# Latent attention scores in three f16 products, and the product with V one head later, in a hybrid attention encoder

## The reference

```python
def mixer_layer(x, c, ...):
    mod = silu(c) @ w_ada + b_ada                     # shift, scale, gate
    h = rms_norm(x, g_norm) * (1 + scale) + shift
    q_lat, kv_lat, k_rope, z_a, q_b, k_b, v_b, z_b = split(h @ w_in)
    # group A: 8 latent heads, 64 + 32 (rotary, shared key) deep, V of 64
    qa = rotate_last_32(rms_norm(q_lat, g_qa) @ w_uq)
    k_nope, va = split(rms_norm(kv_lat, g_kva) @ w_ukv)
    ka = concat(k_nope, rotate(k_rope))
    oa = softmax(qa @ ka.T * MLA_SCALE) @ va
    # group B: 8 query heads on 2 key heads of 64, q and k normalised, 2-D rotary
    ob = softmax(qb @ kb.T * GQA_SCALE) @ vb
    out = concat(oa * silu(z_a), ob * silu(z_b)) @ w_out
    return x + gate * out
```

## Time and profile before

| | |
|---|---|
| median of 3 runs | 2541.19 us (2537.12 to 2541.44) |
| the profiled execution's own time | 2537.28 us |
| its span, first to last instruction | 2535.5 us |
| mean granted TensorE clock | 0.977 of full |
| PE, DVE, ACT, POOL busy | 92%, 54%, 38%, 31% |
| key stages of q = 1 and q = 3, about | 125 and 140 us |
| tile stages of q = 1 and q = 3, 8 tiles each, about | 736 and 752 us |
| tile stages of q = 0 and q = 2, 4 tiles each, about | 304 and 238 us |

### The profile page before, as it was taken

The page is one execution under the profiler, slowest core; times in us unless marked ns, Lnnn a source line. Parts: engine busy times, 40 slices in busy tenths (PEclk is TensorE's granted clock), DMA queues, the critical chain, the costliest instruction groups (busy, mean ns, idle before and its releaser), DMA issues.

```text
span 2535.5 us, 44397 instructions
## 1 busy us (share of the span) xinstructions
PE 2341.6 (92%) x16106; PEld 1392.5 (55%) x16106; DVE 1371.3 (54%) x2444; ACT 974.1 (38%) x2202; POOL 790.5 (31%) x1325
## 2 busy tenths in 40 slices
PE   3888998899999999999989899889999999999997
PEld 1445544456556656656545455445556666665654
DVE  3645454566555555556535444446566555555563
ACT  0233333225444444444422333422354444444442
POOL 0553221664222122123036432146533113212210
PEclk7999999999999999999999999999999999999999
DMA  8712112120000000000412000132000000000001
GB/s 285 253 42 67 50 67 86 50 100 10 18 17 8 25 17 18 16 17 17 165 59 92 18 26 8 42 110 108 9 11 25 17 33 25 8 33 25 0 26 42
DMA packets 63236, 129.43 MB, mean 51 GB/s; under 512 B 6690, under 2 KB 31368, under 8 KB 63132
## 3 DMA queue, kind: packets, MB, share of 16 engines
q1 hardware_dynamic: 63136, 128.09, 14.5%
HBM read 115.44 MB, written 12.63 MB: 51 GB/s over the span
## 4 chain that ended last, share of the span: by engine, by line
PE 72%; DVE 16%; issue 5%; ACT 2%; POOL 2%; DMA 2%; SPq 1%; DVEq 0%; POOLq 0%; ACTq 0%
PE psum L600 55%; PE psum L590 10%; PE psum L808 6%; DVE region L1071 3%; DVE nmax L1054 3%; DVE hT L910 3%; ACT region L1225 1%; POOL region L1279 1%; DVE region L1029 1%; DVE KTa L872 1%; DMA Wout<-in_w_ada 1%; DVE region L1080 1%; PE psum L610 1%; PE psum L594 0%; DVE region L1031 0%
## 5 line engine op out<-in xcount | busy, mean ns | idle before, releaser
L1225 ACT ACTIVATE region<-psum 128x512 f16<-128x512 f32 x640 | 353.5, 594 | 758.5 <-PE psum L590 758.3
L600 PE MATMUL psum<-Wq,hT 128*128 128x512 f32 (+1 forms) x1536 | 611.1, 544 | 6.6 <-DVE KTa L872 5.0
L1071 DVE TENSOR_TENSOR region<-psum,region 128x512 f16<-128x512 f32 x640 | 415.7, 683 | 293.4 <-ACT region L1225 292.7
L590 PE MATMUL psum<-ident,region 128*128 128x128 f32 (+1 forms) x3208 | 436.9, 277 | 25.6 <-DVE Va L966 10.5
L600 PEld LDWEIGHTS psum<-Wq,hT 128*128 128x128 f32 x1536 | 285.0, 191 | 251.2 <-issue 224.9
L1054 DVE TENSOR_REDUCE nmax<-psum 128x1 f32<-128x1024 f32 (+1 forms) x384 | 398.7, 1038 | 40.0 <-PE psum L600 39.0
L590 PEld LDWEIGHTS psum<-ident,region 128*128 128x128 f32 (+1 forms) x3208 | 356.4, 140 | 109.7 <-issue 78.4
L600 PE MATMUL psum<-Wout,region 128*128 128x512 f32 x768 | 354.3, 606 | 9.2 <-DVE region L1039 6.8
L600 PE MATMUL psum<-KTa,region 96*128 96x512 f32 x640 | 312.9, 604 | 18.6 <-DVE region L1029 12.9
L1279 POOL TENSOR_TENSOR region<-region,rope_sb 128x64 f32<-128x64 f32 (+3 forms) x384 | 158.3, 434 | 332.5 <-DVE region L1025 316.1
L1217 ACT ACTIVATE region<-psum,nmax,unscale 128x1024 f32<-128x1024 f32 (+1 forms) x192 | 204.4, 1065 | 142.1 <-DVE nmax L1057 141.6
(11 more groups left out here) (110 smaller groups left out, 2107.8 us busy)
## 6 DMA issues: line engine op xcount, KB each, us to landing
Wout<-in_w_out SPq DMA_DIRECT2D x8, 2048.0 KB, 9.4
Va<-in_w_ada SPq DMA_DIRECT2D x12, 1024.0 KB, 5.4
Wq<-in_w_in SPq DMA_DIRECT2D x6, 2048.0 KB, 15.2
xn<-x_after_layer SPq DMA_DIRECT2D x24, 512.0 KB, 3.3
xn<-in_x_sample SPq DMA_DIRECT2D x16, 512.0 KB, 3.2
Wq<-in_w_ada SPq DMA_DIRECT2D x3, 2048.0 KB, 13.1
Wout<-in_w_ada SPq DMA_DIRECT2D x3, 2048.0 KB, 13.6
x_after_layer<-region SPq DMA_DIRECT2D x12, 512.0 KB, 2.6
```

The lines of the kernel that those rows point to most:

```text
L590: return nc.tensor.transpose(out, in_, ident[0:n, 0:n])
L600: last = nc.tensor.matmul(out, lhsTs[k], rhss[k], start=k == 0, stop=k == n - 1)
L1071: nc.vector.tensor_tensor(PT[:, 1, pt_block(h, S, 4 * c):pt_block(h, S, 4 * c) + 4, :], psum[:, T_BANK + b, :].rearrange("p (c n) -> p c n ...
L1225: nc.scalar.activation(PT[:, 0, pt_block(h, S, 4 * c):pt_block(h, S, 4 * c) + 4, :], psum[:, T_BANK + b, :].rearrange("p (c n) -> p c n", ...
```

## The change

K and Q of group A are kept as f16 high and low parts, scaled by powers of two, and the scores are three f16 products: high by high, low by high, high by low. The scales come from bounds on weights, gains and modulation, taken before the first key step, for which SP loads more weights there. VectorE scales the maxima of group A back as it did those of group B, and the exponential takes the scale. For 1024 keys `mix(h - 1)` stands behind `turn(h)`, ahead of the side products and the scores of slot h, and P^T has two buffers. The core of the diff:

```diff
-        KTa = sb("KTa", [QK, HEADS, SMAX])
+        KTa = sb("KTa", [QK, 2, HEADS, SMAX], F16)
...
-        QTa = part(region1, HEADS * P).rearrange("p (h n) -> p h n", h=HEADS)
+        QTa = part(region1, HEADS * P).bitcast(F16).rearrange("p (a h n) -> p a h n", a=2, h=HEADS)
...
-        PT = part(region2, SMAX).bitcast(F16).rearrange("p (a c n) -> p a c n", a=2, c=SMAX // P)
+        PT = part(region2, 2 * SMAX).bitcast(F16).rearrange("p (a c n) -> p a c n", a=2, c=2 * SMAX // P)
...
         def pt_block(h, S, c):
 
-            return c + (h % 2 * S // P if 2 * S <= SMAX else 0)
+            return c + h % 2 * S // P
...
-                    if part == 1:
+                    if part == 1 and l:
                         sp.dma_start(Wuq[:, :, :], w_uq[l].rearrange("(k p) n -> p k n", p=P)).then_inc(s["wuq_loaded"], 16)
...
                 sp.dma_start(up_v[:, l, :, :], w[:, :, 1, :]).then_inc(s["v_weights_loaded"], 16)
+                sp.dma_start(up_k[:, l, :, :], w[:, :, 0, :]).then_inc(s["v_weights_loaded"], 16)
...
                 sp.dma_start(in_v[:, l, :, :], w[:, :, C_ZB - KVH * GD:C_ZB]).then_inc(s["v_weights_loaded"], 16)
+                sp.dma_start(in_rope[:, l, :, :], w[:, :, C_ZA - ROPE:C_ZA]).then_inc(s["v_weights_loaded"], 16)
+            sp.dma_start(Wuq[:, :, :], w_uq[0].rearrange("(k p) n -> p k n", p=P)).then_inc(s["wuq_loaded"], 16)
+            sp.dma_start(up_q1, w_uq[1].rearrange("(k p) n -> p k n", p=P)).then_inc(s["v_weights_loaded"], 16)
...
-                            last = product(out[:, keys], [QTa[0:QK, h, :]], [KTa[:, h, keys]])
+                            last = product(out[:, keys], [QTa[0:QK, a, h, :] for a in (0, 1, 0)],
+                                           [KTa[:, a, h, keys] for a in (0, 0, 1)])
...
                         turn(h, i)
 
                         side_first = delay or any("^T" in name or "_up" in name for name in before_mix)
+                        if not delay and (h or not first):
+                            mix(h - 1, i)
                         if side_first:
...
-                        if h or delay == 0 or not first:
-                            mix(h - delay, i)
+                        if delay and (h or not first):
+                            mix(h - 1, i)
                         for name in after_mix:
                             side(name, i)
-                    if last and delay:
+                    if last:
                         mix(2 * HEADS - 1, i)
...
-            dve.wait_ge(s["v_weights_loaded"], 16 * 2 * DEPTH)
+            dve.wait_ge(s["v_weights_loaded"], 16 * (4 * DEPTH + 1))
+            dve.wait_ge(s["wuq_loaded"], 16)
             nc.vector.tensor_reduce(rinv[:, 0, 4:6], up_v, AX_XY, ALU.max, apply_absolute_value=True)
+            nc.vector.tensor_reduce(rinv[:, 0, 6:8], up_k, AX_XY, ALU.max, apply_absolute_value=True)
+            nc.vector.tensor_reduce(rinv[:, 2, 0:2], Wuq[:, :, :], AX_X, ALU.max, apply_absolute_value=True)
+            nc.vector.tensor_reduce(rinv[:, 2, 2:4], up_q1, AX_X, ALU.max, apply_absolute_value=True)
+            nc.vector.tensor_reduce(maxima[:, 6:8], in_rope, AX_XY, ALU.max, apply_absolute_value=True)
...
-                            last = nc.vector.tensor_copy(KTa[:, 4 * c:4 * c + 4, tokens(t)],
-                                                         ps[0:QK, :].rearrange("p (h n) -> p h n", h=4))
+                            last = split(KTa[:, 0, 4 * c:4 * c + 4, tokens(t)], KTa[:, 1, 4 * c:4 * c + 4, tokens(t)],
+                                         ps[0:QK, :].rearrange("p (h n) -> p h n", h=4), a_scale[0:QK, l, r:r + 1])
...
-                        last = nc.vector.tensor_copy(QTa[0:QK, 4 * c:4 * c + 4, :], blocks[0:QK])
+                        last = split(QTa[0:QK, 0, 4 * c:4 * c + 4, :], QTa[0:QK, 1, 4 * c:4 * c + 4, :], blocks[0:QK],
+                                     a_scale[0:QK, l, 2:3])
...
-                    if h >= HEADS:
-                        then(last)
-                        last = nc.vector.tensor_scalar(nmax[:, h:h + 1], nmax[:, h:h + 1], unscale[:, l:l + 1], None, ALU.mult)
+                    then(last)
+                    back = unscale[:, l:l + 1] if h >= HEADS else a_unscale[:, l, r:r + 1]
+                    last = nc.vector.tensor_scalar(nmax[:, h:h + 1], nmax[:, h:h + 1], back, None, ALU.mult)
...
-                    scale = 1.0 if h < HEADS else unscale[:, l:l + 1]
+                    scale = a_unscale[:, l, r:r + 1] if h < HEADS else unscale[:, l:l + 1]
```

More of the change, by code:

```diff
@@ L165, in encoder @@
         g_scale = sb("g_scale", [P, DEPTH, 2])
+        a_bound = sb("a_bound", [P, DEPTH, 3])
+        a_scale = sb("a_scale", [P, DEPTH, 3])
+        a_unscale = sb("a_unscale", [P, DEPTH, 2])
         unscale = sb("unscale", [P, DEPTH])
@@ L269, in encoder @@
             .rearrange("p (k n) -> p k n", k=KD)
-        mod1_rows = KTa[0:2, :, SEQS[0]:]
+        mod1_rows = KTa[0:2, :, :, :].rearrange("p a h n -> p (a h n)").bitcast(F32) \
+            .rearrange("p (a h n) -> p a h n", a=2, h=HEADS)[:, :, :, ADA1_N:]
         def ada1_column(i, j):
@@ L1111, in tile @@
                         final_rows(i - 1)
-                key_steps(dve, NT, dict(rounds=(rounds, PER_KEY), own=(own, 3)), key_step, 4 if q == 0 else 2)
+                key_steps(dve, NT, dict(rounds=(rounds, PER_KEY), own=(own, 5)), key_step, 4 if q == 0 else 2)
                 if q == 0:
-                    dve.wait_ge(s["bias1_loaded"], 16 * 4)
+                    dve.wait_ge(s["bias1_loaded"], 16 * 6)
                 row_max(0, 0)
                 row_max(1, 0)
-                over_tiles(dve, NT, dict(rounds=(rounds, PER_SIDE + (len(ADA) if q == 0 else 0)), own=(own, HEADS + (len(ADA) * (ADA_GROUPS - 1) if q == 0 else 0))), tile)
+                over_tiles(dve, NT, dict(rounds=(rounds, PER_SIDE + (len(ADA) if q == 0 else 0)), own=(own, 2 * HEADS + 2 + (len(ADA) * (ADA_GROUPS - 1) if q == 0 else 0))), tile)
                 outputs(1, NT - 1)
```

59 lines of the change are left out of this document (43 added, 16 removed).

## The result

The changed kernel took 2631.14 us (median, 2629.52 to 2631.64) where the kernel before took 2539.15 beside it: a ratio of 1.036, 95% interval 1.0344 to 1.0377, or +92 us. The forecast was +68, 2605 us: the sign was right and 2631 lies inside its range of 2532 to 2635, near the upper end. The profiled executions differ by 93.8 us of span (2629.3 against 2535.5).

What follows compares the result with a forecast made beforehand. Matmuls were taken to set most of the time, with PE waiting on DVE to free the one SIDE bank; 24 + 8 + 5 + 22 + 8 + 1 = +68 us on 2537.3 gives 2605 us, range 2532 to 2635.

Steps and rivals of the forecast that it cites:

- rival C: Scores: f16 products on 96 rows are no faster than the f32 ones; 2630 us, 5% chance.
- D: Scores: f16 records paced faster than 0.2 us, saving more in slots 0, 1 and 3 alone; 2584 us, 1% chance.
- Rival B: Tiles: what PE saves covers what DVE adds, so +36 us only; 2573 us, 15% chance.
- The split: K^T and Q^T leaving PSUM by two dependent DVE instructions: +0.9 us over the copy, bounds 0.7 and 1.1, 96 splits.
- The maximum of a head of group A: Maximum on DVE, now with scaling and a wait: +0.24 us per head, exponential later by that, 192 heads.
- The tile of 1024 keys: Middle tile +2.3 us as savings go into SIDE waits, first +0.5, last -2.2; two stages +24 us.
- Only some 2 us are left in which PE waits: Middle tile of 1024 keys: about 90.4 of 92.4 us is matmuls, so removable stalls are worth 2 us.
- Rival A: PE sets the pace after all, so the scores' 69 us and 28 of stalls come off; 2476 us, 15% chance.
- Key steps: Key stages: two splits exceed DVE's 1.54 us idle per step, about 14 steps x 0.35, +5 us.
- The drains: Drain steps: two splits ahead of each of three PE waits, 5.4 us per instance, four instances, +22 us (17 to 26).
- The start: Before the first key product: extra weight loads on full DMA engines, +8 us, bounds 6 and 14.
- The tiles of 512 keys: Chains grow by split and scaling, some 2.4 us in each of four middle tiles, first and last about -0.5; +8 us.

Runs made afterwards that it cites:

- e1: Changed kernel with the product with V back in its own slot for 1024 keys, f16 scores and splits kept; 2616.5 us.
- e3: Changed kernel without the low parts of group A's K^T and Q^T, the three f16 products all taking high parts; 2564.8 us.
- e4: Changed kernel with VectorE moving side products out before P^T's low part and the maximum, for 1024 keys; 2596.1 us.
- e11: Kernel before (f32 scores) with the later product with V and VectorE's new order, side products first and maximum before gates, for 1024 keys; 2497.9 us.
- e9: Changed kernel with two PE waits in each instance's last drain step filled by four unused f32 products each; 2622.2 us.
- e5: Changed kernel with 28 unused transpositions of the identity in two places of each instance's last drain step; 2689.7 us.
- e10: e8 with unused products filling PE's waits in the drains and before each instance's first key product; 2537.7 us.
- e8: Changed kernel with VectorE's side products first, maximum before gates, and ScalarE making high parts of K^T and the first tile's Q^T; 2532.7 us.

## Why the prediction was right, and where it was off

**The sign and the mechanism** were right. PE's pace is set by when DVE frees SIDE; the 3.4 us of matmuls saved per tile went into those waits. e1, e3 and e4 show each piece of it. The size of the total proves little by itself: 2631 is also what rival C had (2630), and only the rows below tell the two apart.

**The prices.** f16 records of 96 rows are 0.215 us apart (six in 1.29, three in 0.65), so rivals C and D are out. Rival B wanted a middle tile near 92.4 and is out by the 95.38. The Trainium skill's TensorE: Matmul & The Clock Gate has 131 ns for 512 columns (Back-to-back issue gap); no stretch at full clock here comes near it. The split: the next DVE instruction starts at 954.00, 1.43 us after 952.57, where the copy was 0.60, so +0.83 for the +0.9 taken. The maximum of a head of group A: 1.38 us to DVE's next start where the earlier trace rows has 1.14, +0.24 as taken.

**The tile of 1024 keys.** +2.3 predicted, +3.0 in q = 1 and +1.9 in q = 3. Slot 12 is 8.50 us where it was 6.96, +1.54 for +1.55; slot 2's chain is 4.8 for 4.7; slots 14 and 15 together 9.31 for 8.95, as q_a^T1's split waits behind P^T too. The prediction took one tile for both instances, but that of q = 3 was 93.45 long before. The first and last tiles came to -2.6 for -3.4, and two middle tiles are 1.7 us longer than the others, at a lower clock (last section). The term is +30 for +24.

**"Only some 2 us are left in which PE waits"** was right though the trace lists 0.5 of it: e11 runs the same matmuls in 90.66 us, against my 90.4. The rest had been inside the durations, as where a `mix` shows 1.12 in place of 0.86 in the earlier trace rows. Rival A, that PE sets the pace, failed by DVE's order: the 2 us were there to be had, and e11 has them. With f16 scores that order gets a tile to 89.8 us, with 1.7 us of waits for the splits and the move of y_a^T left in it; A needs 87.0 (92.4 - 3.4 - 2).

**Key steps** are 10.35 us where they were 9.99 (10.3 to 10.4 had been said), but only in ten of them, all for 1024 tokens, where 14 had been counted; the others stayed at 9.8 to 9.9 or are first steps. **The drains'** three waits are 2.65, 3.65 and 3.58 us in q = 1, where before they are 0.77, 1.97 and 1.90 (the first and the third are the earlier trace rows): +1.9, +1.7 and +1.7 for +1.8 each. Key steps and drains are +34.5 together, or +23 without the clock's +12, for +27.

**The start** was +8.2 for +8, so 4.1 us for the large pieces and 3.0 or more for the small ones fit as far as the sum can say, and no run took them apart. The Trainium skill's DMA: Bandwidth & Descriptors (Why small descriptors are slow) had given the estimate of 7.2 us, which is not told apart from the +8 either.

**The step that failed** is the one that is not in the sum: the waits were priced at their length, and what PE does behind them at the old clock. By the accounting the lower clock costs 65 us in the changed kernel and 41 before, +24, which is the difference between +68 and +92; of this the fillings of e9 show 9. That the two agree so well is partly luck: without the clock's column the four stages are +11, +23, +12 and +24 for +8, +27, +8 and +24, errors that cancel, and the -3 of the start stands in a stretch that the DMA was said to pace. The tiles of 512 keys carried most of it as an error (+21 for +8): their middle tiles grew by 2.5 and 2.7 us as worked out (+2.4), but the first and last ones, which I had at -0.5 each, run at the lower clock in part and came to +11 together.

**Not seen at all** was that DVE's order was written for the old place of the product. The prediction has the queue of slot 12 in its order and asks what the split adds to it, and not which of its entries had just become free to move.

## What to carry to other kernels

When work is moved later on one engine, look at once for what it lets the other engines put off: here the later product with V and the new order on VectorE cost 11 and 10 us alone and give 43 together. A single buffer that several products share is released by a queue, so price a longer copy by the chain from release to release and not by the engine's busy share: taking away 72 us of VectorE's work, on an engine busy 57%, gave 66 us, some 12 of them through the clock. And price a wait of TensorE with the clock behind it, above all where it comes several times.

## What the runs showed of the hardware that I had not expected

- The granted clock fell to 1.2 GHz behind each of the eight waits of 3.5 to 3.7 us in the changed kernel's drains, and mostly stayed there for some 6 us of matmuls. Behind shorter waits it went either way. Of the waits of 1.5 to 2.5 us, the clock was under 0.9 in the mean of the 3 us behind 6 of 11 in the key stages before, 4 of 7 in the tile stages before, all 5 in the key stages after and 8 of 23 in the tile stages after. In the middle tiles of 1024 keys the wait of 1.90 us once per tile left it at 1.00 in nearly all, and twice (one tile in each of q = 1 and q = 3) such a wait was followed by 5.4 us for products that take 3.7. So the length of the wait alone doesn't decide it here.
- TensorE's program can stall by itself. In e5 (224 transpositions more than the changed kernel has) each middle tile of the last instance has two waits that nothing releases, where its loop begins again:

```profile
2053.94 0.47 PE L608 MATMUL psum<-ident,region 128*128 128x128 f32 x1 [3.70 <-issue]
2057.98 1.75 PE L608 MATMUL psum<-ident,region 128*128 128x128 f32 x7 [3.57 <-issue]
```

  With the clock that falls behind them a tile takes 104 to 108 us in place of 95. e10 has them in two tiles of the execution that was traced, at some 10 us each, which would fit its spread; its other executions were not traced. The code added lies ahead of these loops and not in them, and past the start neither e8 nor the changed kernel has such a wait of 0.9 us or more. What decides it, the length or the place of the program, stays open.
